# Reordered work in the front half of a hybrid-decoder step: two queues for the S5 rows, GELU ahead on ScalarE, dt's chain in pieces, one low part freed early

## The reference

```python
xn = rmsnorm(x) * norm_mix;  proj = xn @ w_in             # -> z, xbc, dt_raw, u
xbc = silu(causal_conv4(xbc))                             # prefix: state of 3 rows for the samples
dt  = softplus(dt_raw + dt_bias)
y   = ssd_chunked(xs, dt, -exp(a_log), B, C, D, h0)       # prompt: chunks of 128; samples: one step
y_ssd = rmsnorm(y * silu(z))
y_s5  = s5(u)                                             # 64 groups of 16 channels, complex diagonal recurrence
y_s5  = gelu(y_s5); y_s5 = rmsnorm(y_s5 * sigmoid(y_s5 @ w_glu + b_glu))
x = x + concat(y_ssd, y_s5) @ w_out
x = x + moe(rmsnorm(x))                                   # 4 groups x 8 experts, top-2 of one group, d_ff 512
y = rmsnorm(x)                                            # and the new conv, SSD and S5 states
```

## Time and profile before

| | |
|---|---|
| time, median of 3 runs | 1016.68 us (1006.02 to 1017.29) |
| the profiled execution's own time | 1019.88 us |
| its span (first to last instruction) | 1018.0 us |
| PE busy | 922.2 us, 91% |
| DVE, ACT, POOL busy | 491.6, 306.4, 227.7 us |
| mean granted TensorE clock | 0.97 |
| DMA, 266.39 MB read and 23.58 MB written | mean 277 GB/s |
| projections, SSD, S5, GLU | 0 to about 400 us |
| output projection | about 400 to 504 us |
| router and first gather | about 504 to 536 us |
| experts | about 536 to 985 us |
| last sums and norm | about 985 to 1018 us |

### The profile page before, as it was taken

How to read it: one execution, slowest core, us unless ns; L and a number is a source line. 1 busy time by engine, 2 the same in 40 slices (tenths; PEclk the granted TensorE clock), 3 DMA queues, 4 the chain that set the end, 5 groups by cost and what they waited for, 6 DMA issues and landing times.

```text
span 1018.0 us, 16758 instructions
## 1 busy us (share of the span) xinstructions
PE 922.2 (91%) x6345; PEld 672.0 (66%) x6345; DVE 491.6 (48%) x856; ACT 306.4 (30%) x641; POOL 227.7 (22%) x468
## 2 busy tenths in 40 slices
PE   8999999989998999999989999999999888788870
PEld 7889878878896688999864555555555444445440
DVE  6999997254545888965352222222222221221136
ACT  3025322263323776423321121212212111111224
POOL 0100788888510111000001111111111101101103
PEclk9999989899999899999999999999999999999995
DMA  7576063033359755657599999989999999999976
GB/s 280 129 144 100 22 118 101 23 106 103 117 119 238 232 186 195 214 175 266 198 405 391 423 423 426 390 329 426 424 423 425 421 427 423 422 428 421 423 295 252
DMA packets 88356, 281.56 MB, mean 277 GB/s; under 512 B 37312, under 2 KB 56720, under 8 KB 70488
## 3 DMA queue, kind: packets, MB, share of 16 engines
q1 hardware_dynamic: 77632, 253.96, 67.0%
q0 software_dynamic: 8480, 19.60, 5.9%
q10 hardware_dynamic: 2176, 7.04, 1.9%
HBM read 266.39 MB, written 23.58 MB: 285 GB/s over the span
## 4 chain that ended last, share of the span: by engine, by line
PE 58%; DMA 20%; DVE 15%; issue 3%; ACT 2%; SPq 1%; POOL 0%; POOLq 0%; ACTq 0%; DVEq 0%
DMA sb_arena<-w_up 16%; PE ps L720 16%; PE ps L974 9%; PE ps L1111 8%; PE ps L1095 8%; PE ps L1086 7%; DVE sb_arena L1517 6%; PE ps L1045 2%; DMA sb_arena<-ssm_in 2%; DVE sb_arena L1526 1%; PE ps L812 1%; DVE sb_arena L2094 1%; DVE sb_arena L1650 1%; DVE sb_arena L1642 1%; DMA sb_kxf<-x_scr,sb_tok_of 1%
## 5 line engine op out<-in xcount | busy, mean ns | idle before, releaser
L720 PE MATMUL ps<-sb_arena 128*128 128x260 f32 (+2 forms) x1152 | 269.0, 395 | 2.5 <-DVE sb_arena L1551 2.3
L720 PEld LDWEIGHTS ps<-sb_arena 128*128 128x128 f32 x1152 | 222.4, 195 | 49.5 <-issue 6.4
L1111 PE MATMUL ps<-sb_arena 128*64 128x512 f32 x544 | 127.6, 612 | 18.4 <-DVE sb_arena L2094 18.4
L1095 PE MATMUL ps<-sb_arena 128*64 128x256 f32 x1088 | 123.9, 380 | 14.1 <-DMA sb_arena<-w_up 14.1
L1086 PE MATMUL ps<-sb_arena 128*64 128x256 f32 x1088 | 123.9, 380 | 10.7 <-issue 10.7
L2090 DVE TENSOR_TENSOR sb_s5b<-sb_s5b,ps 128x256 f32<-128x256 f32 x36 | 22.4, 623 | 219.8 <-PE ps L1095 219.1
L1086 PEld LDWEIGHTS ps<-sb_arena 128*64 128x64 f32 x1088 | 83.3, 137 | 61.2 <-issue 32.5
L662 POOL DMA_INDIRECT out_scr<-sb_kxf,sb_rwc x36 | 35.7, 992 | 389.8 <-DVE sb_kxf L2107 388.9
L1095 PEld LDWEIGHTS ps<-sb_arena 128*64 128x64 f32 x1088 | 78.6, 137 | 55.6 <-DMA sb_arena<-w_up 19.6
L1491 ACT ACTIVATE sb_kxf<-ps,sb_gate_of 64x512 f32<-64x512 f32 x36 | 24.5, 682 | 264.6 <-PE ps L1111 264.5
L1111 PEld LDWEIGHTS ps<-sb_arena 128*64 128x64 f32 x544 | 37.5, 139 | 86.6 <-issue 59.9
(11 more groups left out here) (326 smaller groups left out, 1142.6 us busy)
## 6 DMA issues: line engine op xcount, KB each, us to landing
sb_arena<-w_gate SPq DMA_DIRECT2D x32, 2048.0 KB, 24.2
sb_arena<-w_up SPq DMA_DIRECT2D x31, 2048.0 KB, 27.4
sb_arena<-w_down SPq DMA_DIRECT2D x31, 2048.0 KB, 23.4
sb_arena<-wi SPq DMA_DIRECT2D x27, 512.0 KB, 4.3
sb_arena<-w_out SPq DMA_DIRECT2D x16, 512.0 KB, 4.2
sb_arena<-cs_scr ACTq DMA_DIRECT2D x4, 1024.0 KB, 4.9
sb_arena<-ssm_in POOLq DMA_DIRECT2D x8, 512.0 KB, 9.3
sb_arena<-wglu SPq DMA_DIRECT2D x8, 512.0 KB, 5.4
```

The lines of the kernel that those rows point to most:

```text
L720: last = mm(ps[:, b0 + h, 0:t1 - t0], ring[w % 3][:, k, :], src[:, k, t0:t1], start=k == 0, stop=k == KD - 1)
L1095: last = mm(ps[64 * r:64 * r + 64, 1, 0:256], xt[:, k, :], Wu[i][:, k, 256 * r:256 * r + 256], start=k == 0, stop=k == KD - 1)
L1111: last = mm(ps[64 * r:64 * r + 64, 4, :], ht[:, k % 2, 64 * (k // 2):64 * (k // 2) + 64], Wd[j][:, k, 512 * r:512 * r + 512], start=k == 0 ...
```

## The change

All of it but the last part lies ahead of the output projection; the amount of arithmetic stays the same.

1. Start: 13 warm-up products instead of 9; the mean-square matmuls move from behind block 0 to behind the first k-step of block 1; DVE's partial sum of tiles 4 and 5 comes after the last product with the gains.
2. conv: the two copies for the new conv state leave DVE; `raw_evac` on ACT makes them from PSUM, ahead of its `wide_free` signal.
3. dt: block 13 comes before the ten small matmuls; conv(5), conv(6), conv(7) are put between pieces of the softplus chain; ACT has raw_evac(13) and conv_silu(3) ahead of the exponential, and raw_evac(16) ahead of its wait for the samples' B C sums.
4. First chunk: the samples' dt goes ahead of the samples' S5 step on DVE; ACT has conv_silu(10) ahead of decays(0) and conv_silu(11) behind it, both ahead of segment_exp(0).
5. S5 rows: of each half ACT issues the four transfers with odd j (`y_store_odd`, in chunk 3's part of ACT's program), SP the other five.
6. POOL waits for the second half's stores ahead of the broadcast and states 0 and 1, instead of ahead of states 2 and 3.
7. DVE: sample_c(0), sample_c(1) move behind chunk 3's y and state; sample_update(0), (1) into chunk 4, ahead of its masks; sample_c(2) to (5) stay before chunk 4's y.
8. ACT: the GELUs come ahead of decays(4), sample_decay, b_tokens(4) and segment_exp(4); each waits until block 27 has read the tile that it overwrites (`src_free`); z_evac(27) is between GELU 3 and 4.
9. Output projection: blocks 14 and 15 are computed in the order 14 high-high and high-low, 15 high-low, 14 low-high, 15 high-high and low-high; expert 1's w_down is issued when the low activations are done with.

```diff
-            ydst = y_scr[:, 0:NP_].rearrange("(g c) (j m) -> j c g m", c=C5, j=J)
-            ysdst = y_scr[:, NP_:N].rearrange("(g c) b -> c g b", c=C5)
-
             def y_store(half):
                 sp.wait_ge(y5_ev, 8 * half + 8)
                 gs = slice(32 * half, 32 * half + 32)
-                for j in range(J):
+                for j in range(0, J, 2):
                     sp.dma_start(ydst[j][:, gs], Ug[16 * j:16 * j + 16, gs, 0:NC5]).then_inc(y5_st[half], 16)
                 sp.dma_start(ysdst[:, gs], Ug[0:16, gs, COL_S0:COL_S0 + NS]).then_inc(y5_st[half], 16)
...
             sp.wait_ge(x1t_ev, 6)
             x1_store(512, 768)
+            sp.wait_ge(src_free, KD)
+            sp.dma_start(Wd_to[1], dsrc[1]).then_inc(wd_ld[1], 16)
             sp.wait_ge(o_mm, 16)
-            sp.dma_start(Wd_to[1], dsrc[1]).then_inc(wd_ld[1], 16)
             sp.dma_start(Wg[2], gsrc[2]).then_inc(wg_ld[2], 16)
             sp.wait_ge(x1t_ev, 10)
...
             pl.wait_ge(bc_st, 16)
             pl.wait_ge(s5_out, 32)
+            pl.wait_ge(y5_st[1], 16 * 9)
             pl.dma_start(bcf, bc_scr.rearrange("b c -> (b c)").partition_broadcast(P)).then_inc(bc_ld, 16)
             for b in range(2):
                 pl.dma_start(h0b[b], hin[b]).then_inc(h0s_ld[0], 16)
             pl.wait_ge(bc_ld, 16)
             pl.wait_ge(h0s_ld[0], 32)
-            pl.wait_ge(y5_st[1], 16 * 9)
             for b in range(2, 4):
                 pl.dma_start(h0b[b], hin[b]).then_inc(h0s_ld[0], 16)
...
                     if w == 28:
                         pe.wait_ge(gelu_done, k + 1)
+                    if w == 1 and k == 1:
+                        pe.wait_ge(sum_done, 1)
+                        mean_square(sq0, ms_done, None, 2)
                     for h, (t0, t1) in enumerate(HALVES if w < 20 else HALVES_T):
                         last = mm(ps[:, b0 + h, 0:t1 - t0], ring[w % 3][:, k, :], src[:, k, t0:t1],
                                   start=k == 0, stop=k == KD - 1)
+                    if w == 27 and k < KD - 1:
+                        last.then_inc(src_free, 1)
                 last.then_inc(wide_done, 1)
             def mean_square(src, done, each, tiles=KD):
...
             pe.wait_ge(dve, 1)
-            for _ in range(9):
+            for _ in range(13):
                 mm(ps[:, 6, 0:P], ones[:], ones[:], start=True, stop=True)
             wide(0)
-            pe.wait_ge(sum_done, 1)
-            mean_square(sq0, ms_done, None, 2)
             for w in range(1, 8):
                 wide(w)
             v_transposes(0)
...
             last.then_inc(dt_mm, 1)
             wide(12)
+            wide(13)
             pe.wait_ge(dt_ev, 1)
             for i, (t0, n) in enumerate(TT):
                 last = mm(ps[0:n, 6, i * HEADS:(i + 1) * HEADS], dt_part[:, t0:t0 + n], dt_sel, start=True, stop=True)
             last.then_inc(dtt_mm, 1)
-            wide(13)
             wide(14)
             pe.wait_ge(silu_done, 4)
             for i in range(4):
...
             project_block(12, ((0, 2), (1, 5)))
             project_block(13, ((2, 2), (3, 5)))
-            project_block(14, ((4, 2), (5, 5)))
-            project_block(15, ((6, 5),))
+            def products(o, parts_, opens, closes, turns=()):
+                yh, yl, wh, wl = y_hi[1], y_lo[1], wo_hi[o], wo_lo[o % 3]
+                of = {"hh": (wh, yh), "hl": (wh, yl), "lh": (wl, yh)}
+                for k in range(KD):
+                    for d, at in turns:
+                        if at == k:
+                            x1_turn(d)
+                            logits(d)
+                    for j, name in enumerate(parts_):
+                        w_, y_ = of[name]
+                        for h in range(2):
+                            last = mm(ps[:, 2 * (o % 2) + h, 0:HALF], w_[:, k, :], y_[:, k, HALVES_T[h][0]:HALVES_T[h][1]],
+                                      start=opens and k == 0 and j == 0, stop=closes and k == KD - 1 and j == len(parts_) - 1)
+                return last
+            pe.wait_ge(wo_hid, 15)
+            pe.wait_ge(o_ev, 13)
+            products(14, ("hh", "hl"), True, False, ((4, 2), (5, 5)))
+            pe.wait_ge(wo_hid, 16)
+            pe.wait_ge(o_ev, 14)
+            products(15, ("hl",), True, False).then_inc(src_free, 1)
+            pe.wait_ge(wo_lod, 15)
+            products(14, ("lh",), False, True).then_inc(o_mm, 1)
+            pe.wait_ge(wo_lod, 16)
+            products(15, ("hh", "lh"), False, True, ((6, 5),)).then_inc(o_mm, 1)
             pe.wait_ge(sqt_done, 3)
             pe.wait_ge(o_ev, 15)
             for i, (t0, n) in enumerate(TR):
...
                 act_(dst[:, 3 + SPLIT:3 + NP_], ps[:, b0 + 1, 0:SPLIT], ACT.Copy)
                 sm = dst[:, 531:563].rearrange("p (b j) -> p b j", j=CONV)
-                act_(sm[:, :, 3], ps[:, b0 + 1, SPLIT:N - SPLIT], ACT.Copy).then_inc(wide_free[w % 2], 1)
+                act_(sm[:, :, 3], ps[:, b0 + 1, SPLIT:N - SPLIT], ACT.Copy)
                 f = conv_tile(i)
+                act_(ncp[:, f, :], ps[:, b0 + 1, SPLIT - 3:SPLIT], ACT.Copy)
+                act_(ncs[:, f], ps[:, b0 + 1, SPLIT:N - SPLIT], ACT.Copy).then_inc(wide_free[w % 2], 1)
                 act_(sm[:, :, 0:3].rearrange("p b j -> p j b"), scv[:, :, f, :], ACT.Copy).then_inc(raw_done, 1)
...
             raw_evac(19)
             conv_silu(9)
+            conv_silu(10)
             decays(0)
+            conv_silu(11)
             def segment_exp(c):
...
             segment_exp(0)
-            conv_silu(XBC - 2)
-            conv_silu(XBC - 1)
             ac.wait_ge(ds_ev, 1)
             act_(eA[:], eA[:], ACT.Exp).then_inc(ea_out, 1)
...
                 last.then_inc(hdec_done, 1)
+            def y_store_odd(half):
+                ac.wait_ge(y5_ev, 8 * half + 8)
+                gs = slice(32 * half, 32 * half + 32)
+                for j in range(1, J, 2):
+                    ac.dma_start(ydst[j][:, gs], Ug[16 * j:16 * j + 16, gs, 0:NC5]).then_inc(y5_st[half], 16)
             z_evac(20)
             for c in range(4):
+                if c == 3:
+                    y_store_odd(0)
                 if c:
                     segment_exp(c)
                 b_tokens(c)
+                if c == 3:
+                    y_store_odd(1)
                 ac.wait_ge(l_exp, 4 * c + 4)
                 spread(c + 1)
                 for w in ((21, 22), (23, 24), (25,), (26,))[c]:
                     z_evac(w)
-                    if w % 2 or w == 26:
+                    if w in (21, 23, 25):
                         decays(c + 1)
-            sample_decay(0)
-            sample_decay(1)
-            z_evac(27)
-
-            b_tokens(4)
-            segment_exp(4)
-            for i in range(8):
+            def gelu(i):
                 if i % 4 == 0:
                     ac.wait_ge(yraw_ld[i // 4], 16)
+                if i < 7:
+                    ac.wait_ge(src_free, i + 1)
+                else:
+                    ac.wait_ge(wide_done, 28)
                 act_(yg[:, i, META:NP_].rearrange("p (m j) -> p j m", j=J),
                      yraw[:, i, 0:NP_].rearrange("p (j m) -> p j m", j=J)[:, :, META // J:], ACT.Gelu_apprx_tanh)
                 act_(yg[:, i, NP_:N], yraw[:, i, NP_:N], ACT.Gelu_apprx_tanh).then_inc(gelu_done, 1)
+            for i in range(4):
+                gelu(i)
+            z_evac(27)
+            for i in range(4, 8):
+                gelu(i)
+            sample_decay(0)
+            decays(4)
+            b_tokens(4)
+            sample_decay(1)
+            segment_exp(4)
...
             ts(sp_u, dvf, -1.0, None, ALU.mult)
             V.tensor_tensor(sp_u, sp_u, dvf, ALU.min).then_inc(s5_dve, 1)
...
             tt(spz, sps, sps, ALU.mult)
             link(V.memset(sp_u, 1.0 / 17))
-            for m in (15, 13, 11, 9, 7, 5, 3):
+            for m in (15, 13):
                 tt(sp_u, sp_u, spz, ALU.mult)
                 ts(sp_u, sp_u, 1.0 / m, None, ALU.add)
+            conv(6)
+            for m in (11, 9, 7, 5, 3):
+                tt(sp_u, sp_u, spz, ALU.mult)
+                ts(sp_u, sp_u, 1.0 / m, None, ALU.add)
+            conv(7)
             tt(sp_u, sp_u, spz, ALU.mult)
             ts(sp_u, sp_u, 1.0, 2.0, ALU.add, ALU.mult)
...
                 conv(i)
+            dv.wait_ge(ds_mm, 1)
+            link(V.tensor_copy(dts[:], ps[:, 6, 256:256 + 64].rearrange("p (i b) -> p i b", i=8)))
+            tt(eA[:], dts[:], bc(aexp[:], 2, NS), ALU.mult)
+            ts(eA[:], eA[:], -1.0, None, ALU.mult)
+            dv.wait_ge(silu_done, XBC)
...
                 if 0 < c < 4:
                     off_diagonal(c, n)
+                if c == 4:
+                    for b in range(2):
+                        sample_update(b)
                 for g in range(2):
                     dv.wait_ge(l_exp, 4 * c + 2 * g + 2)
                     V.tensor_tensor(Lm[0:n, 8 * g:8 * g + 8, 0:n], Lm[0:n, 8 * g:8 * g + 8, 0:n],
```

(15 more changed lines are left out.)

37 lines of the change are left out of this document (17 added, 20 removed).

## The result

The changed kernel took 1019.11 us (median of 20 runs, 1015.5 to 1024.44), the kernel before 1014.41 in the same comparison (20 runs, 1006.02 to 1021.87): ratio 1.0046, 95% interval 1.0027 to 1.0065. It is slower by 4.7 us where 10.1 us of gain were forecast, and 1019.11 lies outside the range of 997 to 1018. Yet its profiled execution took 1016.59 us for a span of 1014.8, 3.3 less than the profiled one of before. Two questions follow: why 3.3 and not 10.1 from profile to profile, and why a loss between the medians.

The account below looks back on a forecast made before the run. TensorE was taken to set when the last 308 us of weight stream start, so front savings reach the end one for one. 8.2 us at the output projection plus 1.9 made 10.1: 1019.9 to 1009.8 profiled, 1006.6 median; range 997 to 1018.

Parts of the forecast that it names:

- Start: Block 0: four more warm-ups fill TensorE's 2.35 us wait so it runs warm; gain 0.4 us, bounds -0.3 and +0.9.
- dt: Around L795: block 13 first hides a 2.11 us wait, saving 5.6; a new 2.4 us wait before block 16; net 3.2.
- first chunk: ssd_a(0)'s 4.23 us wait and cold costs go, 7.0 us; new wait of 1.9 to 2.0 before block 21; net 5.1.
- GpSimd's recurrence: Needed by the S5 outputs, not waited for before; if now late, some us of the 8.7 gained would be lost there.
- S5 rows: Each half's stores need 8.8 us of packets; second half done, and broadcast issued, at 311.8 us.
- Samples' transfers: Broadcast and states after the rows: 5.3 MB, 12.5 us, and 1; sample_c(0) starts at 325.3 against 323.88.
- The chain behind sample_c(0): Through state 2's store and ACT's sigmoids: 67.2 us to the output projection, starting at 392.5, 8.2 us earlier.
- Low part: Output projection to experts: earlier w_down lets the first gather meet less traffic; gain 1.9 us, bounds 0 and 3.6.
- Rival 1: Samples' transfers overlap better: sample_c(0) at 319, output projection at 386.2, time 998.6 us; chance 0.15.
- Rival 2: S5 row stores take as long as before: sample_c(0) at 339.8, output projection at 407.0, time 1021.1 us; chance 0.10.
- deciding point, 335.4: A sample_c(0) start after 335.4 us would decide for the slower case, row stores as long as before; chance 0.10.
- Rival 3: TensorE's clock falls in new waits before block 16 and block 21, about 2.6 us each: 1011.8 us; chance 0.15.

Follow-up runs that it names:

- e14: The kernel before, unchanged, profiled a third time; its profiled execution took 1012.27 us, span 1010.5.
- e1: The changed kernel, unchanged, measured and profiled a second time: 1019.1 us, ratio 1.0020 to the kernel before.
- e3: The changed kernel with SP's ring loads 31 and 32 issued ahead of its wait for chunk 4's state: 1017.66 us, ratio 1.0005 to the kernel before.
- e4: The kernel before with only the start, conv copies, dt and first-chunk parts of the change: 1011.10 us, ratio 0.9949 to the kernel before.
- e11: The kernel before with one edit, POOL waiting for the second half's rows ahead of the broadcast: 1037.92 us, ratio 1.0167.
- e7: The kernel before with the parts up to the first chunk plus reordered blocks 14 and 15 and earlier w_down: 1008.33 us, ratio 0.9935.
- e10: The changed kernel with POOL's wait back behind states 0 and 1, and ring loads 31 and 32 issued earlier: 1013.34 us, ratio 0.9927 to before.

## Why the prediction was wrong

**Start, dt, first chunk: right against the profile that the sum was made on, in part no gain against the medians.** The two old waits went, the new ones were 1.75 (forecast 2.4) and 1.83 (1.9). From place to place the gains were 0.3 at the start, 3.4 at dt and 5.1 at the first chunk (forecast 0.4, 3.2 and 5.1). Another 1.4 came in blocks 17 to 19 (23.63 us instead of 24.38, and what stands just ahead of them), where nothing was changed: that is luck of the two executions. Together TensorE was 10.2 us ahead at the S5 outputs (8.7).

But 8.3 of those 10.2 are also had by the kernel before in the execution of e14. The dt term's "L795 takes half" (1.0) and "blocks 13 and 14 take 14.6 instead of 17.05" (2.5) were taken from one execution, and the sum took the same 10.1 us off the median as off the profile. Of these 3.5, e14 had 3.2 already. Block 21's 1.3 is another matter: e14 paid most of it, and the changed kernel (7.25 us) did not. Before's 35 runs beside e1 show the same from outside: 12 had a mean clock of 0.974 or more and took 1014.8 on average, 15 had 0.970 or less and took 1020.1. The changed kernel's 32 runs (the 20 of the comparison and e1's 12) took 1018.5 (17 runs) and 1021.5 (6 runs) at the same two clocks: 3.6 more than before where the clock is high, 1.4 more where it is low. These runs come from two comparisons and show an association, not its cause; e1's 12 alone do not follow the clock (1019.3 and, in two runs, 1019.2). The clocks of before's 20 runs in the first comparison are not on record; their median of 1014.4 is that of the runs with the high clock.

That GpSimd's recurrence might become late was named in the prediction; it now does, by 0 to 1.7 us (e1).

**S5 rows: right to 1 us** (12.5 against 12.4; broadcast issued at 312.38 against 311.8).

**Samples' transfers: the step that failed.** "These are 5.3 MB, 12.5 us, and 1" priced broadcast and states at 13.5 us; they took 17.8. The bytes were not far off (5.9 MB, w_out's first loads among them), but they moved at 330 GB/s and not at 424. The trace of before already had the group from issue to use, 305.2 to 323.9 us, 18.7, and it took 17.5 to 19.5 in every kernel. With 17.8 in the sum sample_c(0) comes at 311.8 + 17.8 = 329.6, with the rows 0.6 late at 330.2; it came at 330.20. Why this mix of transfers moves at 330 GB/s is not shown.

**The chain behind sample_c(0): one path missing.** Forecast 67.2 us to the output projection, by the store of state 2 and ScalarE's sigmoids. Measured 71.1 (73.0 in e1). SP's ring load 31 is queued behind its wait for chunk 4's state, which VectorE reaches behind sample_c(2) to (5). With it ahead of the wait the chain took 68.0 (e3). The two errors, 4.9 at sample_c(0) (4.3 of them the transfers) and 3.9 behind it, are the 8.8 us between 392.5 and 401.3, and 8.2 of gain became a loss of 0.6.

**Low part: right** (2 us against 1.9). From profile to profile the way from the output projection to the end shortened by 3.8 us, and so 0.6 of loss there became a gain of 3.3 in the spans. But 1.7 of it is one tile, the down matmuls of the first expert tile, which took 5.35 us in the two slower profiles of before and 3.65 in e14, e4 and e11, without the low part.

**Rivals.** Rival 1 (sample_c(0) at 319) did not come. Rival 2 named the right place, sample_c(0), but the wrong mechanism: the stores did get shorter. Its deciding point, 335.4, was also computed on the profile with the poor clock. Against e14, where sample_c(0) starts at 314.87 and the output projection at 394.94, the changed kernel loses 6.4 us at the projection and gets 2 back from the low part: 4.3 in the spans (1014.8 against 1010.5), which is close to the 4.7 between the medians. Rival 3 (new waits drop the clock) was seen in some executions: in e3, e7 and e10 the clock fell behind waits of 3.3, 2.8 and 3.2 us before block 16, and block 16 took 8.9 to 9.2 us instead of 7.5; behind 1.5 to 1.75 us it did not. It isn't what decides.

**Left open:** why the second queue and the new orders cost 0.4% each alone and nothing together (each one's wait is shown, their interplay is not), and what lets the clock fall behind a 2.1 us wait, or with no wait at all at 188 us, in one execution and not in another.

## What to carry to other kernels

Price a transfer by the time from issue to use of that very transfer in the trace, not by bytes at the best rate: this group took 17.5 to 19.5 us with the row stores beside it or not, so making it wait its turn only added to the path. Before a gain is taken from rows at a low clock, profile the old kernel several times; a wait of 2.1 us cost its own length in one execution here and more than twice that in another, and only the first is surely gained. When one queue's program holds a weight load behind a wait for another engine's late result, that load is part of every chain through that engine.

## What the hardware showed that was not expected

- The 2064 KB broadcast landed 12.2 us after issue beside the row stores, and 12.3 us with the stores already out; the second half's stores, in turn, took 16.1 and 16.8 us on one queue without it and 21.5 to 23.1 beside it.
- Four strided stores issued by ScalarE held it 4.0 us while the rows were alone and 13.0 to 13.1 us beside the broadcast.
- Behind the same wait (2.11 and 2.13 us) the granted clock fell in two profiles of the same kernel and stayed in a third: 3.0 us. At 188 us it fell to 0.50 in the first profile of before with TensorE busy for the 50 us ahead, and stayed at 1.00 in e14: another 3.1.
- Broadcast, states and what ran beside them moved at 330 GB/s with a DMA share of 0.95, where the experts' stream moves 424 at 1.01.
